# Min of the gate and product of gate and up on GpSimd, up's clamp kept in two buffers on VectorE

## What is computed

```python
def expert_block(args):
    xb, e = args
    gu = xb @ w_gate_up[e] + b_gate_up[e]
    gate, up = gu[:, :D_EXPERT], gu[:, D_EXPERT:]
    gate = jnp.minimum(gate, SWIGLU_LIMIT)
    up = jnp.clip(up, -SWIGLU_LIMIT, SWIGLU_LIMIT)
    act = (up + 1) * (gate * jax.nn.sigmoid(SWIGLU_ALPHA * gate))
    return act @ w_down[e] + b_down[e]
```

## Time and profile before

| | us |
|---|---|
| median of three runs | 1645.24 (1644.16 to 1646.59) |
| the profiled execution's own time | 1642.67 |
| its span in the trace | 1640.8 |
| TensorE busy | 1605.7 (98%) |
| VectorE busy | 1343.3 (82%) |
| ScalarE busy | 1051.9 (64%) |
| GpSimd busy | 436.4 (27%) |

### The profile page before, as it was taken

One profiled execution on the slowest core, in us unless ns is written; L12 is line 12 of the kernel. 1 busy time (PEld: TensorE's weight loads), 2 busy tenths in 40 slices (PEclk: granted clock), 3 DMA queues, 4 the chain that ended last, 5 costly groups with the idle time before them and its releaser, 6 DMA issues.

```text
span 1640.8 us, 24160 instructions
## 1 busy us (share of the span) xinstructions
PE 1605.7 (98%) x7853; PEld 1319.3 (80%) x7853; DVE 1343.3 (82%) x1050; ACT 1051.9 (64%) x912; POOL 436.4 (27%) x287
## 2 busy tenths in 40 slices
PE   8999999999998989999999999999999999999997
PEld 6797777788896768888888888888888888888885
DVE  6974555523658879999999999999999999999995
ACT  5533444422346667777877777777787777777874
POOL 0000000501103643343422234232343323333230
PEclk8999999999999999999999999999999999999999
DMA  7331222333367889999999999999999999999993
GB/s 246 116 103 52 77 77 77 114 99 109 125 250 275 338 307 379 365 379 387 388 383 370 379 391 387 379 376 377 386 389 381 376 379 384 386 386 377 373 377 124
DMA packets 117210, 476.92 MB, mean 291 GB/s; under 512 B 17005, under 2 KB 60249, under 8 KB 67879
## 3 DMA queue, kind: packets, MB, share of 16 engines
q1 hardware_dynamic: 104612, 456.59, 73.3%
q0 software_dynamic: 12560, 19.81, 4.8%
HBM read 469.78 MB, written 23.83 MB: 301 GB/s over the span
## 4 chain that ended last, share of the span: by engine, by line
PE 93%; DVE 4%; issue 1%; ACT 1%; DMA 0%; POOLq 0%; ACTq 0%; SPq 0%; DVEq 0%
PE ps L657 29%; PE ps L659 29%; PE ps L658 29%; PE ps L897 2%; DVE work L1471 2%; PE ps L766 1%; PE ps L786 1%; PE ps L775 1%; PE ps L926 1%; PE ps L932 0%; DVE zT L1347 0%; DMA r<-in_x 0%; DVE r L1479 0%; PE ps L846 0%; DVE w_lo L1347 0%
## 5 line engine op out<-in xcount | busy, mean ns | idle before, releaser
L1347 DVE TENSOR_TENSOR zT<-raw,zT 128x2048 fp32r<-128x2048 f32 x96 | 217.6, 2295 | 52.3 <-ACT zT L1020 52.3
L1788 POOL DMA_INDIRECT r<-expert_inputs_by_quarter,quarter_at x124 | 215.1, 1734 | 52.7 <-issue 28.6
L1347 DVE TENSOR_TENSOR w_lo<-more_raw,w_hi 128x2048 fp32r<-128x2048 f32 x96 | 217.6, 2294 | 4.0 <-ACT w_hi L1020 2.1
L1347 DVE TENSOR_TENSOR zT<-more_raw,zT 128x2048 fp32r<-128x2048 f32 x96 | 219.9, 2292 | 1.1 <-ACT zT L1020 1.1
L1020 ACT ACTIVATE w_hi<-raw 128x2048 fp32r<-128x2048 f32 x96 | 184.4, 1922 | 52.4 <-PE ps L659 42.3
L1347 DVE TENSOR_TENSOR w_lo<-raw,w_hi 128x2048 fp32r<-128x2048 f32 x96 | 215.8, 2274 | 1.1 <-issue 1.0
L657 PE MATMUL ps<-zT,xT 128*128 128x512 f32 x512 | 203.6, 398 | 3.8 <-DVE zT L1347 3.8
L657 PE MATMUL ps<-w_hi,xT 128*128 128x512 f32 x512 | 201.3, 393 | 5.4 <-DVE xT L1664 2.7
L1020 ACT ACTIVATE zT<-more_raw 128x2048 fp32r<-128x2048 f32 x96 | 184.2, 1919 | 34.0 <-PE ps L659 30.4
L659 PE MATMUL ps<-zT,xT 128*128 128x512 f32 x512 | 200.2, 391 | 0.0
L658 PE MATMUL ps<-zT,xT 128*128 128x512 f32 x512 | 200.2, 391 | 0.0
(11 more groups left out here) (275 smaller groups left out, 3166.2 us busy)
## 6 DMA issues: line engine op xcount, KB each, us to landing
more_raw<-in_w_gate_up SPq DMA_DIRECT2D x129, 1024.0 KB
raw<-in_w_gate_up SPq DMA_DIRECT2D x127, 1024.0 KB
raw<-in_w_down SPq DMA_DIRECT2D x65, 1024.0 KB
more_raw<-in_w_down SPq DMA_DIRECT2D x63, 1024.0 KB
raw<-in_w_in SPq DMA_DIRECT2D x29, 1024.0 KB, 5.3
r<-in_x SPq DMA_DIRECT2D x8, 512.0 KB, 6.3
raw<-in_w_branch_conv SPq DMA_DIRECT2D x4, 1024.0 KB, 5.0
raw<-in_w_out SPq DMA_DIRECT2D x4, 1024.0 KB, 4.9
```

What stands on the lines that cost most here:

```text
L1347: nc.vector.tensor_tensor(expert_pair(1, c), chunk, expert_pair(0, c).bitcast(F32), ALU.subtract).then_inc(split_lo, 2)
L1788: nc.gpsimd.indirect_dma_start(out=quarters[:, part, :], out_offset=None, in_=h2_quarters, in_offset=bass.IndirectOffsetOnAxis(ap=quarter_ ...
```

## The change

`up_part` keeps only the clamp, which now writes half 0 to `u1b` and half 1 to a second buffer (both named in the list `up_kept`). GpSimd gets a function `product(g)`: for each half it waits for the gate activation, takes the minimum with the limit in place (`tensor_scalar`), waits for that and for up's clamp, and multiplies into act (`tensor_tensor`), which counts `act_ok` up. `product(before)` stands in GpSimd's round between the gathers and the copy ahead of the scatter, and once more behind the loop, for the last block. Block 0 keeps its own VectorE code.

```diff
             def up_part(g, half):

                 ve.wait_ge(used, unit_base(g) + 16)
-                ve.wait_ge(act_ok, 2 * g + (half + 1))
-                nc.vector.tensor_scalar(u1b, ps[:, bk_B + half, :], 1.0 + LIMIT, 1.0 - LIMIT, ALU.min,
+                ve.wait_ge(act_ok, 2 * g + half)
+                nc.vector.tensor_scalar(up_kept[half], ps[:, bk_B + half, :], 1.0 + LIMIT, 1.0 - LIMIT, ALU.min,
                                         ALU.max).then_inc(up_clamped, 1)
-                ve.wait_ge(up_clamped, 2 * g + (half + 1))
-                ve.wait_ge(sigmoid_ok, 2 * g + (half + 3))
-                ve.wait_ge(turned_pe, tile(g, half))
-                nc.vector.scalar_tensor_tensor(act[:, half, :], sgb[half], GATE_TOP, u1b, ALU.min,
-                                               ALU.mult).then_inc(act_ok, 1)
...
+            gp.sem_inc(gate_clamped, 2)
+
+            def product(g):
+
+                for half in range(2):
+                    gp.wait_ge(sigmoid_ok, 2 * g + (half + 3))
+                    gp.sem_inc(gp_step, 1)
+                    nc.gpsimd.tensor_scalar(sgb[half], sgb[half], GATE_TOP, None, ALU.min).then_inc(gate_clamped, 1)
+                    gp.wait_ge(gate_clamped, 2 * g + (half + 1))
+                    gp.wait_ge(up_clamped, 2 * g + (half + 1))
+                    gp.wait_ge(turned_pe, tile(g, half))
+                    nc.gpsimd.tensor_tensor(act[:, half, :], sgb[half], up_kept[half], ALU.mult).then_inc(act_ok, 1)
+
...
                 gather_next(g)
+                product(before)
                 scatter(g, 2 * before, 2 * before + 2)
                 stored(before)
...
                 turn_round(before)
+            product(but_one)
             scatter(nblk, 2 * but_one, 2 * nblk)
```

More of the change, by code:

```diff
@@ L331, in hybrid_block @@
         u1b, sgb = work[:, 1024:1536], [work[:, 1536:2048], work[:, 2048:2560]]
-        u_first = [u1b, work[:, 3584:4096]]
+        up_kept = [u1b, work[:, 3584:4096]]
         hot = work[:, 2560:2560 + EARLY * 256].bitcast(BF16).rearrange("p (e b n) -> p e b n", e=EARLY, b=NB)
@@ L416, in hybrid_block @@
         up_clamped, sigmoid_ok = sem("up_clamped"), sem("sigmoid_ok")
+        gate_clamped = sem("gate_clamped")
         act_ok = sem("act_ok")
@@ L1685, in first_up @@
                 ve.wait_ge(used, unit_base(0) + 16)
-                nc.vector.tensor_scalar(u_first[half], ps[:, bk_B + half, :], 1.0 + LIMIT, 1.0 - LIMIT, ALU.min,
+                nc.vector.tensor_scalar(up_kept[half], ps[:, bk_B + half, :], 1.0 + LIMIT, 1.0 - LIMIT, ALU.min,
                                         ALU.max).then_inc(up_clamped, 1)
@@ L1692, in first_act @@
                 ve.wait_ge(up_clamped, half + 1)
-                nc.vector.scalar_tensor_tensor(act[:, half, :], sgb[half], GATE_TOP, u_first[half], ALU.min,
+                nc.vector.scalar_tensor_tensor(act[:, half, :], sgb[half], GATE_TOP, up_kept[half], ALU.min,
                                                ALU.mult).then_inc(act_ok, 1)
```

## The result

The changed kernel took 1802.62 us (median of 4, 1800.55 to 1804.67) against 1644.7 us before: ratio 1.0967, 95% interval 1.0951 to 1.0983. The prediction was 1669 us with a range of 1650 to 1704. The direction was right; the size was off by a factor of more than six (158 us lost where 24 were forecast), so the mechanism that I priced is not the one that decides. The profiled execution took 1804.67 us, its span 1802.8.

A forecast was written before the change was run, and what follows sets the result against it. TensorE was taken as the bound, full in its 34.36 us rounds. A late second product costs 0.8 us in each of 30 rounds, 24 us on 1645.2, giving 1669 us, range 1650 to 1704.

The forecast's parts named there:

- the sentence on the other queues: GpSimd's copy and scatter stand behind the product; the scatter comes 4 us later, only the next store waits: no cost.
- the loop's far half: A late TensorE delays its end of round, ScalarE's store, chunk 2 and the next second product alike: no recovery.
- The race with chunk 2: GpSimd's second product against VectorE's chunk 2 split, within 0.1 to 0.2 us; lost every round, TensorE 0.8 us late.
- The prices: GpSimd instructions on 512 columns: min 1.4 us, product 1.1 us, with 0.1 to 0.2 us between for semaphores.
- The min's hold on VectorE: GpSimd's min blocks a running VectorE split for 0.42 us, with the whole instruction, 1.4 us, as upper bound.
- The margin of 0.15 us on VectorE: In an early round 0.39 us lost on VectorE cost TensorE 0.24, so VectorE has 0.15 us to spare.
- The first rival: The min holds VectorE for its whole length, so VectorE bounds: 36.1 us a round, 1698 us; chance 0.26, above it 0.05.
- The second: GpSimd's product comes too late for chunk 2 in some rounds only; with half lost 12 us, 1657 us; chance 0.11.
- The third: GpSimd's min runs at the cast's rate, 0.47 us; rounds stay 34.36 us, 1645 us; chance 0.09, faster 0.02.
- VectorE's relief: Two products leave VectorE, freeing 1.53 us per round; worth at most the 2.7 us of small waits, TensorE being full.

The follow-up runs named there:

- The first three experiments: Changed kernel with GpSimd's index copy ahead of the products: 1689.67 us; kernel before with four spare GpSimd instructions ahead of the copy: 1836.95 us, behind it: 1666.8 us.

## Why the prediction was wrong

**The step that failed** is the sentence on the other queues: a scatter delayed by 4 us, "and what waits for that is the next store, 34 us on, so it costs nothing". I followed the scatter and not the copy ahead of it. ScalarE's store waits for `row_column_ok`, which that copy counts up, since it takes its scale from `uix`; the wait stands in `store_y` beside the one for `rows_free`. The store was in the rows that I read, with its 3.46 us wait for TensorE, and I even based the chain on it (store, chunk 2), but looked only at the releaser that had come last in the kernel before. Before, the copy had been done at 923.45, 3.8 us ahead of the store at 927.28. That was its slack, and the four instructions, 8.0 us from 1015.58 to the copy's start in the round shown, used it up. The first three experiments show this: 113 us come back by moving the copy, and spare instructions cost 195 us ahead of it, 24 behind it.

**The loop.** I had the loop's far half right: a late TensorE delays the store, chunk 2, the gathers and the products alike, so lateness stays in every round. Its entry was another one, with more in it: products, copy, store, chunk 2 on two engines, TensorE.

**The race with chunk 2** I took as lost in each round, 0.8 us. In the changed kernel it isn't run at all, as chunk 2 waits for the copy. With the copy first it is lost as forecast, but a round grew by 1.34 us and not by 0.8 (35.70 us), 47 us in all. The wait itself is 1.03 us, because the second product ended 3.7 us behind the start of chunk 2 and not 3.3. The other 0.3 us is longer busy time around the wait (34.66 us in such a round, with the clock at 1.00), which I had put at nothing.

**The prices** held: min 1.49 us where nothing runs beside it (I took 1.4), product 1.29 (1.1), 0.16 between them (I had 0.1 to 0.2). The min's hold on VectorE is 0.42 us, as taken from one row of before; the product's 1.1 (1.0) in the run with the products ahead of all gathers, 3.37 against 2.28, and 1.3 in the run with the copy first.

The margin of 0.15 us on VectorE, which I read from one early round, rests on too little: in the kernel before, a round with no elementwise work on GpSimd took 34.66 us too (1517.07 to 1551.73).

The Trainium skill, SBUF — State Buffer, section Who interferes with whom, has the loser blocked for the whole instruction. The product's hold nearly agrees (1.1 of 1.29 us), the min's doesn't (0.42 of 1.49).

**The first rival**, VectorE as the bound, is refuted: VectorE idles 7.6 us ahead of chunk 2 in a round of the changed kernel. **The second**, a race lost in some rounds only, fails in the run with the copy first, where TensorE waits for the product in each. **The third**, no loss with a short min, fails for the change as well: with no min at all it still lost 74 us, because the copy stood behind the products. Only with the copy first did the shorter chain cost nothing (1640.76 us).

**The clock** was missing. I forecast waits of 0.8 us and no effect on it. At about 3.2 us per round it fell each time, and TensorE was busy 64 us longer, most of it by the clock. At 1.03 us per round, in the run with the copy first, the clock stayed at 1.00 in all but three rounds of the loop. The mean was 0.984, and TensorE was busy 15 us longer in all.

That VectorE's relief is worth nothing but the small waits was right. That the median came out at the same 2.7 us is partly luck, with an interval of 1.0 to 4.3.

What stays open is what decides whether the clock falls behind a wait. The wait's length alone doesn't: in the run without the min it stayed at 1.00 in a round with a wait of 2.23 us and fell in the next with 2.19. No run varied this alone.

## What to carry to other kernels

Before work is put into an engine's program, list every semaphore that the instructions behind it count up, and for each who waits on it and how long ago it was satisfied. Of several waits the profile names only the one that ended last. One that ended earlier is invisible there, and its slack (here 3.8 us of a tiny copy) is the price limit of what is put ahead. Small instructions that release another engine belong ahead of large ones that nobody needs yet. And where the bound engine has no idle time, relieving another can't pay.

## What the runs showed of the hardware

A tiny GpSimd instruction that reads SBUF was held up until VectorE's running two-input instruction had ended. The same 128x2 copy took 0.18 us with VectorE idle (1023.57 in the changed kernel), 0.57 in the run with the spare instructions behind it, and 1.36 in the run with the copy first (980.73), where it ended with the split beside it. The granted clock fell to half in every round with a wait of TensorE of about 3.2 us, for 3.4 or 6.8 us; in the round shown that began 6 matmuls behind the wait. Waits of 2.2 us were followed by a fall in some rounds and not in others, and waits of 1.03 to 1.08 us in 2 of 22 rounds of the run with the copy first. And GpSimd's min of 128x512 took 1.49 us but held VectorE for 0.42 only, while the product of the same size held it for 1.1 of its 1.29 us.
